# Low-rank gates as fp32 products among the first chunks, key chunks in halves, a split modulation side

## The reference, cut to what matters

```python
sh1, sc1, g1, sh2, sc2, g2 = split(silu(c) @ w_ada + b_ada, 6)        # w_ada: 2048 x 12288
sh1c, sc1c, ...            = split(silu(c_ctx) @ w_ada + b_ada, 6)
h_l = rms_norm(x, norm1_w)   * (1 + sc1)  + sh1                       # 256 tokens
h_c = rms_norm(ctx, norm1_w) * (1 + sc1c) + sh1c                      # 256 context tokens
gq, gk, gv, gr, gaf, gab, dq, dk, dv = split(h @ w_in, IN_OFFSETS)    # gk: 512 wide; gaf, gab: 16 each
log_a_f = log_sigmoid(gaf @ w_a_up_f + b_a_f) / 16                    # 16 -> 512
log_a_b = log_sigmoid(gab @ w_a_up_b + b_a_b) / 16
```

## Time and profile before

| | us |
|---|---|
| median of 3 runs | 2362.49 |
| lowest, highest | 2360.41, 2362.8 |
| the profiled execution | 2355.38 |
| its span, first to last instruction | 2353.5 |
| PE busy in it | 2274.7 (97%) |
| DVE, ACT busy | 1467.4, 1037.1 |
| mean granted clock of PE | 0.993 of full |

### The profile page before, as it was taken

How to read it: one execution, slowest core, us unless ns; L and a number is a source line. 1 busy time by engine, 2 the same in 40 slices (tenths; PEclk the granted TensorE clock), 3 DMA queues, 4 the chain that set the end, 5 groups by cost and what they waited for, 6 DMA issues and landing times.

```text
span 2353.5 us, 37737 instructions
## 1 busy us (share of the span) xinstructions
PE 2274.7 (97%) x15705; PEld 2035.0 (86%) x15705; DVE 1467.4 (62%) x2046; ACT 1037.1 (44%) x1409; POOL 45.4 (2%) x57
## 2 busy tenths in 40 slices
...
GB/s 367 377 145 198 230 198 210 139 145 134 144 135 126 195 255 303 290 184 222 229 251 246 222 189 189 181 186 181 186 168 183 158 201 188 132 134 126 126 177 145
DMA packets 249611, 458.64 MB, mean 195 GB/s; under 512 B 18932, under 2 KB 43826, under 8 KB 248033
## 3 DMA queue, kind: packets, MB, share of 16 engines
...
q0 software_dynamic: 2368, 9.56, 1.1%
...
...
## 4 chain that ended last, share of the span: by engine, by line
PE 88%; DVE 4%; DMA 2%; ACT 2%; DVEq 1%; issue 1%; SPq 1%; ACTq 0%
PE psum L636 78%; DMA sbuf<-in_w_ada 2%; PE psum L613 1%; DVE sbuf L1941 1%; PE psum L1038 1%; PE psum L1146 1%; ACT fast L1308 1%; PE psum L707 1%; DVE fast L1893 1%; PE psum L889 1%; PE psum L944 1%; PE psum L1176 1%; PE psum L963 1%; DVEq L1940 1%; SPq L507 1%
## 5 line engine op out<-in xcount | busy, mean ns | idle before, releaser
L636 PE MATMUL psum<-fast,fast 128*128 128x256 f32 (+3 forms) x13536 | 2043.4, 312 | 21.7 <-DVE fast L1893 13.7
L636 PEld LDWEIGHTS psum<-fast,fast 128*128 128x128 f32 (+2 forms) x13536 | 1855.9, 189 | 199.0 <-issue 48.2
L1893 DVE TENSOR_TENSOR fast<-sbuf,fast 128x1024 fp32r<-128x1024 f32 (+5 forms) x669 | 783.2, 1176 | 727.7 <-ACT fast L1308 720.4
L1308 ACT ACTIVATE fast<-sbuf 128x1024 fp32r<-128x1024 f32 (+4 forms) x673 | 680.5, 1017 | 1076.3 <-PE psum L636 966.2
L1941 DVE SCALAR_TENSOR_TENSOR sbuf<-sbuf,sbuf 128x512 f32<-128x512 f32 x210 | 157.8, 751 | 18.9 <-issue 1.3
L1308 ACT ACTIVATE sbuf<-psum 128x256 f32<-128x256 f32 (+5 forms) x189 | 85.3, 476 | 81.7 <-PE psum L636 39.7
L1913 DVE TENSOR_TENSOR fast<-sbuf,fast 128x512 fp32r<-128x512 f32 (+1 forms) x61 | 53.4, 876 | 4.5
L613 PE MATMUL psum<-sbuf,sbuf 128*128 128x128 f32 (+2 forms) x221 | 39.9, 289 | 11.3 <-DMA sbuf<-in_consts 9.6
L613 PEld LDWEIGHTS psum<-sbuf,sbuf 128*128 128x128 f32 (+2 forms) x221 | 26.6, 146 | 22.6 <-DMA sbuf<-in_consts 9.6
L1673 ACT ACTIVATE sbuf<-psum,sbuf 128x256 f32<-128x256 f32 x88 | 44.2, 551 | 0.0
L2315 DVE SCALAR_TENSOR_TENSOR sbuf<-psum,sbuf,sbuf 128x255 f32<-128x255 f32 x88 | 38.4, 478 | 3.3
...
## 6 DMA issues: line engine op xcount, KB each, us to landing
sbuf<-in_w_ada SPq DMA_DIRECT2D x192, 512.0 KB, 5.0
sbuf<-in_w_up SPq DMA_DIRECT2D x176, 512.0 KB, 3.9
sbuf<-in_w_in SPq DMA_DIRECT2D x154, 512.0 KB, 3.9
sbuf<-in_w_down SPq DMA_DIRECT2D x88, 512.0 KB, 4.3
sbuf<-in_w_gate SPq DMA_DIRECT2D x64, 512.0 KB, 3.7
sbuf<-in_w_out SPq DMA_DIRECT2D x64, 512.0 KB, 5.0
sbuf<-in_w_proj_gla SPq DMA_DIRECT2D x16, 512.0 KB, 4.6
sbuf<-in_w_proj_diff SPq DMA_DIRECT2D x16, 512.0 KB, 6.2
```

The lines of the kernel that those rows point to most:

```text
L636: last = mm(out, lhsT, rhs, start=first and key not in opened, stop=end, skip_group_check=True)
L1308: return A(out, in_, ACT.Copy, scale=scale)
L1893: last = tt(lo, raw, hi.bitcast(F32), ALU.subtract)
```

## The change

1. **Low-rank gates.** Job ga is gone. Its weights (`gaw`, fp32, 128x16x32) are loaded by GpSimd's queue near the start. `low_gates(j)` does four fp32 products for the token tiles 2j and 2j + 1, high and low part each, into four groups of 32 rows of bank 7, with 512 columns of tokens. Eight such blocks are spread over the stage. ACT copies the 128 rows once, ahead of its copies of the keys; wup is repeated in four row groups (eight small loads instead of four), and each gate logit is one product with all 128 rows, which sums the four.
2. **Key chunks in halves.** `key_tiles(j, m0, n)` does n of a chunk's four output tiles. `KEYS_AT` gives for each half the modulation chunk behind which it stands; the last two chunks come behind all of them. `KEYS_IN` has all eight key chunks, and earlier: ahead of (2, 2), (2, 5), (3, 4), (4, 4), (5, 6), (6, 2), (8, 2), (9, 0).
3. **Last side in two parts.** Sides are now (0,4), (4,4), (8,4), (12,2), (14,2) in first tile and number of tiles. The last four panels are 256 columns wide, four chunks of four k-tiles each: 64 modulation chunks as before, in ten panels. In the streams of ACT and DVE chunk 2u - 1 is split between the two keeps of side u, and chunk 2u behind the token splits of side u.

```diff
+SIDES = [(0, 4), (4, 4), (8, 4), (12, 2), (14, 2)]
+EARLY = 2 * len(SIDES)
+ADA_COLS = [2048 * part + P * k for k, n in SIDES for part in (0, 1)]
+ADA_WIDTH = [P * n for k, n in SIDES for part in (0, 1)] + [512] * 16
...
-KEYS_IN = {(3, 1): 0, (3, 5): 1, (5, 1): 2, (5, 5): 3, (7, 1): 4, (7, 4): 5}
-KEYS_AFTER = {(3, 4): 0, (3, 7): 1, (5, 3): 2, (5, 6): 3, (7, 3): 4}
...
+KEYS_IN = {(2, 2): 0, (2, 5): 1, (3, 4): 2, (4, 4): 3, (5, 6): 4, (6, 2): 5, (8, 2): 6, (9, 0): 7}
+KEYS_AT = {(3, 3): (0, 0), (3, 4): (0, 2), (3, 6): (1, 0), (3, 7): (1, 2), (4, 6): (2, 0), (4, 7): (2, 2),
...
-        self.add("gk", gk[6:8])
-        self.add("ga", panel("w_in", 3072, 32, kt=16))
...
+            pool.dma_start(gaw, dram["w_in"][:, 3072:3104].rearrange("(k p) n -> p k n", p=P)).then_inc(S("gaw_loaded"), 16)
-            for r in (0, 32):
+            for r in range(0, P, 32):
...
+            def key_tiles(j, m0, n):
+                g = st.job["gk"][j]
+                if m0 == 0:
+                    pe.wait_ge(S("h_ready"), j + 1)
+                    pe.wait_ge(S("weights_split"), st.nth[g] + 1)
+                hi, lo = half(g, 0), half(g, 1)
+                todo = [both_sides(2 * j + k, hi[:, k, :], lo[:, k, :]) for k in range(2)]
+                for m in range(m0, m0 + n):
+                    for k in range(2):
+                        _, out, pairs = todo[k][m]
+                        for x, (lhsT, rhs) in enumerate(pairs):
+                            last = mm(out, lhsT, rhs, start=j == 0 and k == 0 and x == 0, stop=j == 7 and k == 1 and x == 2,
+                                      skip_group_check=True)
+                    if j == 7 and m < 3:
+                        last.then_inc(S("tiles_done"), 1)
+                if m0 + n == 4:
+                    last.then_inc(S("split_multiplied"), 1)
+                    if j == 7:
+                        for b in BANKS["gk"]:
+                            turns[b] += 1
+            def low_gates(j):
+                pe.wait_ge(S("h_ready"), j + 1)
+                if j == 0:
+                    pe.wait_ge(S("gaw_loaded"), 16)
+                    pe.wait_ge(S("tokens_turned_act"), 8)
+                for part in range(2):
+                    for k in (2 * j, 2 * j + 1):
+                        r = 32 * (2 * part + k % 2)
+                        last = mm(cut(bank(7), 2, T)[r:r + 32, :, :], gaw[:, k, :], XR[:, :, part, k, :].bitcast(F32), start=j == 0,
+                                  stop=j == 7, skip_group_check=True)
+                if j == 7:
+                    last.then_inc(S("gates_multiplied"), 1)
...
-                    if (a, i) in KEYS_AFTER:
-                        j = KEYS_AFTER[a, i]
-                        pe.wait_ge(S("h_ready"), j + 1)
-                        gemm_chunk("gk", j, both_sides)
+                    if (a, i) in KEYS_AT:
+                        j, m = KEYS_AT[a, i]
+                        key_tiles(j, m, 2)
+                        if m:
+                            low_gates(j)
...
-            ada_fold(7)
-            for j in range(len(KEYS_AFTER), 8):
-                pe.wait_ge(S("h_ready"), j + 1)
-                gemm_chunk("gk", j, both_sides)
+            key_tiles(6, 0, 1)
+            ada_fold(EARLY - 1)
+            low_gates(6)
+            key_tiles(6, 1, 3)
+            low_gates(7)
...
-                            pe.wait_ge(S("wup_loaded"), 64)
+                            pe.wait_ge(S("gates_copied"), 1)
...
-                            r = slice(32 * (j % 2), 32 * (j % 2) + 32)
-                            mm(bank(6 + j % 2), wup[r, d, (j % 4) * P:(j % 4 + 1) * P], ga[r, :], start=True, stop=True
+                            mm(bank(6 + j % 2), wup[:, d, (j % 4) * P:(j % 4 + 1) * P], ga, start=True, stop=True
...
-            for q in (1, 2, 3):
-                rows_copy(2 * q)
-                round_chunk(2 * q - 2)
-                round_chunk(2 * q - 1)
-                rows_copy(2 * q + 1)
-                if q == 3:
-                    round_chunk(6)
-                modulate(q)
-            for s in (7, 8, 9):
+            round_chunk(0)
+            for u in range(1, len(SIDES)):
+                rows_copy(2 * u)
+                round_chunk(2 * u - 1)
+                rows_copy(2 * u + 1)
+                modulate(u)
+                if u < len(SIDES) - 1:
+                    round_chunk(2 * u)
+            for s in (8, 9):
                 round_chunk(s)
+            act.wait_ge(S("gates_multiplied"), 1)
+            copy(ga, bank(7)).then_inc(S("gates_copied"), 1)
...
-            split_tokens(0, 0)
-            split_tokens(0, 1)
-            for q in (1, 2, 3):
-                columns_keep(2 * q)
-                rest_chunk(2 * q - 2)
-                rest_chunk(2 * q - 1)
-                columns_keep(2 * q + 1)
-                gains(q)
-                split_tokens(q, 0)
-                if q == 3:
-                    rest_chunk(6)
-                split_tokens(q, 1)
-            for s in (7, 8, 9):
+            split_tokens(0)
+            split_tokens(1)
+            rest_chunk(0)
+            for u in range(1, len(SIDES)):
+                columns_keep(2 * u)
+                rest_chunk(2 * u - 1)
+                columns_keep(2 * u + 1)
+                gains(u)
+                k, n = SIDES[u]
+                for j in range(k // 2, (k + n) // 2):
+                    split_tokens(j)
+                if u < len(SIDES) - 1:
+                    rest_chunk(2 * u)
+            for s in (8, 9):
...
```

More of the change, by code:

```diff
@@ L171, in __init__ @@
         self.sums_at, self.fold_at, self.keep_at = {}, {}, {}
-        ada = {a: panel("w_ada", c, 512) for a, c in enumerate(ADA_COLS)}
+        ada = {a: panel("w_ada", c, w, kt=SLOT_WORDS // w) for a, (c, w) in enumerate(zip(ADA_COLS, ADA_WIDTH))}
         gk = panel("w_in", 512, 512)
-        for a in range(8):
-            for i in range(8):
+        for a in range(EARLY):
+            for i in range(len(ada[a])):
                 if (a, i) in KEYS_IN:
@@ L189, in __init__ @@
                     + [(f"pd{n}", panel("w_proj_diff", 512 * n, 512, rows=1024)) for n in range(4)]
-                    + [(f"out{n}", panel("w_out", 512 * n, 512)) for n in range(4)], ada, range(16, 20), 15, 8)
+                    + [(f"out{n}", panel("w_out", 512 * n, 512)) for n in range(4)], ada, range(SPREAD, SPREAD + 4), 15, 8)
         ups = [(f"u{'gv'[v]}{i}", panel("w_up", DFF * v + 512 * i, 512)) for i in range(KF // 4) for v in range(2)]
-        self.beside(ups[:KFA // 2], ada, range(20, 24), 5, 2, 14)
+        self.beside(ups[:KFA // 2], ada, range(SPREAD + 4, SPREAD + 8), 5, 2, 14)
         c = KFA * P
@@ L396, in pieces @@
             views = [ring(g), half(g, 0), half(g, 1)]
-            if (w, col) in (("w_in", 3072), ("w_in_2", 1024)):
+            if (w, col) == ("w_in_2", 1024):
                 return [[views[0].unsqueeze(2).to_broadcast([P, kt, 2, width])]
@@ L423, in build @@
         tmp = Y(11280, 2048)
-        ga = Y(11280 + 512, 512)[0:64, :]
+        gaw = Y(11280, KD, 32)
+        ga = Y(11280 + 512, 512)
         qtmp = Y(11280 + 1024, 1024)
-        wup = Y(11280 + 1024, 2, 512)[0:64, :, :]
+        wup = Y(11280 + 1024, 2, 512)
         rows = [Y(13328, 512), Y(22176, 512)]
@@ L702, in ada_chunk @@
                 w = ring(g)
-                for j in range(2):
-                    k = 2 * i + j
-                    for h in range(2):
-                        r = slice(64 * j + 32 * h, 64 * j + 32 * h + 32)
-                        last = mm(bank(ROWS_BANK[a], 0, T)[r, :], csil[:, k, :], w[:, j, T * h:T * h + T], start=k < 2,
-                                  stop=k >= 14, skip_group_check=True)
+                kt, halves = st.chunks[g][2], ADA_WIDTH[a] // T
+                for j in range(kt):
+                    k = kt * i + j
+                    for h in range(halves):
+                        r = 32 * (halves * j + h)
+                        last = mm(bank(ROWS_BANK[a], 0, T)[r:r + 32, :], csil[:, k, :], w[:, j, T * h:T * h + T],
+                                  start=i == 0, stop=k >= KD - kt, skip_group_check=True)
                 last.then_inc(S("plain_multiplied"), 1)
             def ada_fold(a):
-                if a < 8:
+                if a < EARLY:
                     pe.wait_ge(S("ada_rows_copied"), a + 1)
@@ L756, in turn_tokens @@
                     yield
+            def key_tiles(j, m0, n):
[30 more added lines that the diff above has]
+                    last.then_inc(S("gates_multiplied"), 1)
             turning = iter(())
-            for a in range(8):
-                for i in range(8):
+            for a in range(EARLY):
+                for i in range(len(st.job[f"ada{a}"])):
                     ada_chunk(a, i)
@@ L850, in key_norms @@
                     yield
-            gemm("ga", lambda k, hi, lo: [(0, cut(bank(0)[0:64, :], 2, T),
```

(1 more changed line is left out.)

89 lines of the change are left out of this document (46 added, 43 removed).

## The result

| us | before | after |
|---|---|---|
| median, lowest to highest | 2362.64, 2360.41 to 2365.43 | 2385.62, 2383.34 to 2386.93 |
| runs | 4 | 4 |
| the profiled execution; its span | 2355.38; 2353.5 | 2385.08; 2383.0 |
| first product of gv0 | 149.18 | 172.74 |

The ratio after to before is 1.0107, interval 1.0095 to 1.012: the change costs 23.0 us. The forecast was 2381 (+18.7). The two profiled executions differ by 29.7 us (their spans by 29.5), since that of before ran 7 us quicker than its median, which the prediction had put into its sum.

The account below looks back on a forecast made before the run. First stretch bound by w_ada loads, TensorE having little slack. Waits for key-chunk slots, less job ga, +13.4 at gv0, start 2.2, logits 2.1, clock 1.0: +18.7, 2374.1 profiled, 2381 with 7.1 for the median; range 2368 to 2388.

Parts of the forecast that it names:

- The rival that the slots don't bind: Key-load slots come free early enough or the gap is covered; gv0 at 134.7, time 2350; chance 8%.
- The start, +2.2: Gate-weight and extra wup loads on GpSimd's queue near 15 us, while engines are full, delay the start by 2.2 us.
- Steps 1 and 2: Up to panel 3's fold: (3,2) lands at 63.2, gk0 starts at 65.2, fold at 81.8, before the start shift.
- Step 3: Behind panel 3's fold: 8.4 us until gk2 is split, (4,4) lands at 93.9, TensorE idle 10.5 us.
- Step 4: From (4,4) through gk2, a low-rank block and modulation chunks; fold of panel 4 at 105.7.
- Step 5: Behind panel 4's fold: gk3 split at 107.8, (5,5) lands at 111.5, fold of panel 5 at 119.0.
- Steps 6 and 7: Behind panel 5's fold: 8.4 us wait, (7,2) lands at 131.1; TensorE's work then runs to 148.9, loads hidden.
- Step 8: Fold of panel 9 at 150.3, then 12.3 us without a token wait; gv0 starts at 162.6.
- The rival of serial column groups: Low-rank blocks' four column groups don't run side by side, 3.4 us a block; +17 more, 2398; chance 3%.
- the clock: Lower granted clock after TensorE's holes, ahead of gk2 and gk4 on the path; 1.0 us added (0 to 4).
- the old kernel paid the same twice: Said of the lower clock after idles: before paid it too, partly under waiting loads; 1.0 us was added.
- landings at 5.2 us: Loads landing 5.2 us after issue instead of 3.7, counted in the wait chain's own range of +13 to +25.

Follow-up runs that it names:

- e1: Kernel after with only the loading order changed, key chunks loaded later; 2373.03 us, ratio 1.0059 to before.
- e2: Kernel after with key chunks 0, 2 and 4 rounded and split earlier, ahead of the token splits; 2365.86 us, ratio 1.0027 to before.
- e3: Kernel before with only its key chunks loaded earlier; 2378.77 us, ratio 1.0085 to before.
- e4: Kernel after with the gate weights set to zero instead of loaded, products the same; 2385.26 us, ratio 1.011 to before.
- e5: Kernel after with useless products ahead of (3,2), (4,4) and (6,2), where TensorE stood idle; 2382.35 us, ratio 1.0096 to before.

## Why the prediction was right, point by point

**The direction and the mechanism.** The prediction said that the slots of early key chunks, held until VectorE splits them, stop SyncE's queue. e1 and e2 break that from the two sides (later loads, earlier splits), and e3 makes it in the kernel before. SyncE's wait rows changed as was written, and the DMA share fell at 80 to 95, to 0.01 at 110 to 115 and to 0.04 at 134 to 136 us, ahead of (4,4), (5,5) and (7,2). The rival that the slots don't bind is out.

**The start, +2.2.** Measured 54.11 - 51.23 = +2.9 at the fold of panel 1; of the load itself e4 shows 1.0 there and 1.9 at gv0.

**Steps 1 and 2.** With the start added, (3,2) was due at 65.4 and came at 66.27, behind 5.29 idle; the fold of panel 3 was due at 84.0 and came at 87.41. Of these 3.4 us, 2.0 are the first half of gk0 at the lower clock, 5.05 us instead of 3.06 for the second:

```profile
66.27 1.08 PE L713 MATMUL psum<-sbuf,sbuf 128*32 128x256 f32 x8 [5.29 <-DMA sbuf<-in_w_ada]
67.67 1.08 PE L713 MATMUL psum<-sbuf,sbuf 128*32 128x256 f32 x8 [0.31 <-DMA sbuf<-in_w_ada]
68.68 5.05 PE L779 MATMUL psum<-fast,fast 128*128 128x512 f32 x12
...
74.22 3.06 PE L779 MATMUL psum<-fast,fast 128*128 128x512 f32 x12
77.21 1.06 PE L798 MATMUL psum<-fast,sbuf 128*32 128x512 f32 x8
78.09 1.05 PE L713 MATMUL psum<-sbuf 128*32 128x256 f32 x16
```

**Step 3, the wait ahead of (4,4).** 8.4 us from fold to split were forecast, 8.2 came (87.41 to 95.61); 3.7 from issue to product, 3.9 came; idle 10.5, 10.57 came. This is the step on which the forecast rested.

**Step 4.** From (4,4) to the fold of panel 4: 11.8 forecast (105.7 - 93.9), 13.9 came (113.48). The first half of gk2 is 1.7 of the difference, and the chunk ahead of it, 1.08 instead of 0.64, another 0.4.

**Step 5.** From the fold of panel 4 to that of panel 5: 13.3 forecast, 14.2 came. SyncE stood for gk3's slot until about 115.8, and TensorE did gk3 meanwhile, as was written; it had no wait ahead of (5,5) itself.

**Steps 6 and 7 held only in part.** SyncE did stand for gk4's split, 9.7 us, and issued (7,2) at 135.9, 8.2 behind the fold where 8.4 were forecast. But TensorE had no idle before (7,2): it was in the first half of gk4 and reached (7,2) at 142.31. What it waited for instead was (6,2), 3.23 us at 131.50, behind (6,1) and gk5 in the queues; the prediction had left the loads of (6,2) to (7,1) out of its path. The fold of panel 5 came 6.5 us after its forecast of 121.2, and the rest of step 7 added 1.5.

**Step 8.** From the fold of panel 9 to gv0 12.3 us were forecast and 12.32 came (160.42 to 172.74), with no wait for the last tokens:

```profile
160.42 0.51 PE L731 MATMUL psum<-sbuf,sbuf 128*128 128x2 f32 x4
160.85 1.07 PE L798 MATMUL psum<-fast,sbuf 128*32 128x512 f32 x8
161.85 4.39 PE L779 MATMUL psum<-fast,fast 128*128 128x512 f32 x18
166.17 1.06 PE L798 MATMUL psum<-fast,sbuf 128*32 128x512 f32 x8
167.16 5.74 PE L779 MATMUL psum<-fast,fast 128*128 128x512 f32 x24
172.74 3.56 PE L641 MATMUL psum<-fast,fast 128*128 128x512 f32 x15
```

**The unit prices.** A low-rank block is 1.06 us long and its successor begins 0.88 to 1.0 behind its start; 1.0 was taken. The rival of serial column groups is out. Two pairs of gate logits, each 1.88 long, begin 7.20 apart with a chunk between them (178.18 and 185.38), instead of 6.72, so +0.48 each; 0.5 was taken.

**The term that was mis-sized is the clock.** gv0 came at 172.74 against a forecast of 165.8 (162.6 + 2.2 + 1.0), 6.9 us later. The three first halves of gk0, gk2 and gk4 took 5.05, 4.75 and 4.69 us instead of some 3.0: 2.0 + 1.7 + 1.7 = 5.4. The last chunk ahead of each, 1.08 instead of 0.64, and the fold at 136.81, 1.01 instead of 0.61, make 1.7 more, all behind the last wait and so on the path. About 7 us were due where 1.0 was added, beyond the bound of 4. This 7 is an estimate from the rows of after; with the 0.7 by which the start was short it closes the sum to a few tenths. e5 took away the first two of the three, by the same count 4.6, and gave 4.8 at gv0.

The step that failed is the sentence that the old kernel paid the same twice. It paid 1.0 and 2.0 in the earlier trace rows, but with the DMA share at 1.03 to 1.06 all the while the earlier trace rows, so that chunks went on landing; after paid three times, and behind queues that had stopped.

The median moved by 23.0, not by the 23.6 of gv0 and 2 for the logits; a part of that is the scatter behind gv0 that the first section shows. So it is luck that the median missed its forecast by less (4.6 us) than gv0 did. The range up to 2388 held, though the clock went past its bound, since its upper end also allowed for landings at 5.2 us, which did not come.
